# Channel norms: squares per tile on two engines, sums in four strips of the array, root and inverse on a column, tables loaded beside a norm

## Chip, cores and metric

One core of one Trainium2 chip runs the whole program: two layers of one kind of block and one hybrid layer, 256 tokens, width 1024, all in fp32. The metric is the device time of one execution in microseconds (us), less is better. Engines are called TensorE (PE; PEld is its weight load), VectorE (DVE), ScalarE (ACT), GpSimd (POOL) and SyncE (SP).

## The reference

The change touches only the norms over the 1024 channels of each token. In the reference they are:

```python
def rmsnorm(x, g):
    y = xf * lax.rsqrt(jnp.mean(xf * xf, axis=-1, keepdims=True) + NORM_EPS)
    return (y * g.astype(jnp.float32)).astype(x.dtype)

def layernorm(x, g, b):
    mu = jnp.mean(xf, axis=-1, keepdims=True)
    var = jnp.mean(jnp.square(xf - mu), axis=-1, keepdims=True)
    return ((xf - mu) * lax.rsqrt(var + LN_EPS) * g + b).astype(x.dtype)

def modulate(x, g, shift, scale):
    return rmsnorm(x, g) * (1 + scale) + shift
```

Around them stand the mixers (a recurrence over tokens, a convolution, gates), the choice and the weighted sum of 16 x 8 expert rows per token (`peer`), and in the hybrid layer four attention-like branches and an MLP.

## The kernel before

Activations lie with channels on partitions: a tensor of 1024 channels and 256 tokens is 8 tiles of 128 partitions x 256 tokens. The mean over channels is therefore a sum over partitions and tiles, made on TensorE with a 128x128 matrix of ones as the stationary operand; the sum then stands in all 128 partitions.

The program is a row of stages (`k.stage()`, line 82). Each stage opens a block in which every engine has its own list of instructions; at its end all engines meet, and the counters' marks are taken again. Within a stage engines wait for each other only through counters (`multiplied`, `vec_step`, `act_step`). Nothing of one stage runs beside the next, except DMAs and gathers that a stage has issued and not waited for.

`channel_norm` (line 356) is one such stage. ScalarE squares all tiles in one instruction (line 398). TensorE multiplies the 8 tiles of squares by ones into one PSUM bank (line 416). VectorE scales and adds eps over 128x256 (line 381), ScalarE takes the root (400), VectorE the reciprocal (385), and then VectorE multiplies tile by tile (387) while ScalarE follows with gain and shift, tile by tile (404). With `center=True` the mean comes first: 8 matmuls (411), a scaling (374), and one subtraction over all tiles (375). It is called 17 times: in the opening without gain (line 2510), for the mixers (1338) and the experts (1510) with gain and shift, three times centred after the convolution (1318), twice on one or two tiles (2268, 2269), and with a gain alone at 2302, 2365, 2367, 2375 and 2625.

In three places a job of expert rows is hosted beside other work: GpSimd gathers rows into a ring of four (`fetch_rows`, 1462), and VectorE uses a fixed number of them at the start of each stage (`use_rows`, 1440; in a norm four, or two when centred). `k.job` is None where none is hosted.

`gemm` (line 111) multiplies a weight of n blocks with the activations; its first four blocks are fetched by the stage before. Products follow most norms, and cannot start before the norm's stage has ended. In the opening (2479) SP has queued the tables of the modulation, the layer's tables and x before the norm; TensorE then multiplies the modulation's tables with 32-column weights, each of four tables onto its own 32 rows of a PSUM bank, in turn (`multiply`, 270).

`load` (line 345) is a stage of its own: SP issues transfers and waits for them, and all other engines wait at its end. It is used for `final_g` (in `k_final`, 2655), for the second table of constants (program) and for three small tables of the second block (2296).

## Time and profile before

| | us |
|---|---|
| median of 3 runs | 6153.47 |
| lowest, highest | 6142.9, 6162.07 |
| the profiled execution, its own time | 6142.74 |
| its span, first to last instruction | 6140.9 |
| TensorE busy (matmuls) | 3304.5 (54%) |
| VectorE busy | 3687.1 (60%) |
| ScalarE busy | 1000.6 (16%) |
| GpSimd busy | 1843.9 (30%) |
| granted TensorE clock, mean | 0.749 of full |

How to read it: the shares are averages over stages in which different engines work, so no share tells what a stage is bound by. In the page's list of groups, `L416` is the line of the kernel, `x246` the number of records (an fp32 matmul leaves two), then busy us and mean ns of one, and behind the bar how long the engine had been idle before them and whom it had waited for. A timeline shows single instructions (or merged neighbours) in order of time. `PEclk` is the granted clock of TensorE; 1.00 is 2.4 GHz and 0.50 is 1.2 GHz.

### The profile page before, as it was taken

How to read it: one execution, taken by the hardware profiler on the slowest of the kernel's cores; microseconds unless marked ns; L12 is line 12 of the kernel's file. 1: busy time of each engine (PE TensorE's matmuls, PEld its weight loads, DVE VectorE, ACT ScalarE, POOL GpSimd, SP SyncE). 2: the span in 40 equal slices, each digit the busy share in tenths (PEclk: the TensorE clock that was granted, in tenths of full speed). 3: DMA queues.
4: the chain of work that ended last, by engine and by line, in shares of the span. 5: the costliest groups of instructions: out<-in, count | busy, mean ns of one | idle time of the engine just before them, and what ended most of it. 6: DMA issues, size and time to landing. Idle time of an engine off the chain costs nothing. (4 is left out here: it accounts for less than half of the span.)

```text
span 6140.9 us, 90198 instructions
## 1 busy us (share of the span) xinstructions
PE 3304.5 (54%) x34040; PEld 2815.9 (46%) x34040; DVE 3687.1 (60%) x6974; ACT 1000.6 (16%) x2443; POOL 1843.9 (30%) x1550
## 2 busy tenths in 40 slices
PE   7688784887765013666500388878000000745988
PEld 6577673676654012556400367767000000644777
DVE  3556517568876866688799525661887898143110
ACT  1124211113330000233200012431000000111110
POOL 0000001326543750165577300000188776000000
PEclk9899997897687556777655689999555555866999
DMA  6320045767756971477799632003199998200432
GB/s 247 126 70 3 9 144 212 264 223 238 231 196 227 358 257 57 164 246 247 239 370 369 227 103 86 3 9 117 73 331 326 347 373 300 93 0 28 135 114 117
DMA packets 299017, 1117.17 MB, mean 182 GB/s; under 512 B 33696, under 2 KB 39088, under 8 KB 290224
## 3 DMA queue, kind: packets, MB, share of 16 engines
q0 software_dynamic: 221184, 805.40, 36.8%
q1 hardware_dynamic: 77488, 306.90, 14.6%
q8 instruction: 249, 4.08, 0.3%
q14 instruction: 96, 0.79, 0.0%
HBM read 1111.12 MB, written 1.05 MB: 181 GB/s over the span
## 5 line engine op out<-in xcount | busy, mean ns | idle before, releaser
L159 PE MATMUL psum<-h,weight_ring 128*128 128x256 f32 x4672 | 1045.0, 388 | 99.8 <-PEq L85 99.8
L1473 POOL DMA_INDIRECT ring<-in_peer_u,expert x496 | 620.4, 1251 | 1445.5 <-issue 667.4
L159 PEld LDWEIGHTS psum<-h,weight_ring 128*128 128x128 f32 x4672 | 909.5, 195 | 235.1 <-issue 101.0
L1715 DVE SCALAR_TENSOR_TENSOR tok<-ring,act,tok 128x1024 f32<-128x1024 f32 x688 | 884.0, 1285 | 94.1 <-DMA ring<-in_peer_v,expert_group 56.6
L1751 PE MATMUL psum<-constants,tok 128*128 128x128 f32 x48 | 10.7, 417 | 1564.5 <-PEq L85 1564.5
L1667 POOL DMA_INDIRECT ring<-in_peer_v,expert_group x688 | 776.8, 1129 | 219.4 <-issue 209.3
L1751 PEld LDWEIGHTS psum<-constants,tok 128*128 128x128 f32 x48 | 9.8, 225 | 1565.2 <-issue 1565.2
L1453 DVE CUSTOM_DVE_ANT_0 ring<-ring,tok 128x1024 f32<-128x1024 f32 x496 | 598.5, 1221 | 194.8 <-DMA ring<-in_peer_u,expert 175.4
L1667 POOL DMA_INDIRECT ring<-in_peer_u,expert_group x272 | 340.3, 1251 | 739.9 <-DVE expert_group L1703 662.2
L1710 DVE CUSTOM_DVE_ANT_0 ring<-ring,tok 128x1024 f32<-128x1024 f32 x272 | 329.7, 1226 | 85.7 <-DMA ring<-in_peer_u,expert_group 82.6
L159 PE MATMUL psum<-m,weight_ring 128*128 128x256 f32 x768 | 180.7, 401 | 53.5 <-PEq L85 53.5
L159 PEld LDWEIGHTS psum<-m,weight_ring 128*128 128x128 f32 x768 | 155.0, 203 | 79.2 <-issue 55.7
L398 ACT ACTIVATE squares<-x_tokens 128x2048 f32<-128x2048 f32 x7 | 13.4, 1910 | 1088.0 <-PEq L85 1088.0
L1266 PE MATMUL psum<-h,weight_ring 128*128 128x256 f32 x768 | 175.2, 391 | 23.5 <-PEq L85 23.5
L1018 POOL MEMSET W<- 128x1024 f32 x4 | 3.8, 953 | 595.0 <-POOLq L85 595.0
L416 PE MATMUL psum<-squares,constants 128*128 128x256 f32 x246 | 87.2, 529 | 170.9 <-ACT squares L398 170.9
L381 DVE TENSOR_SCALAR row<-psum 128x256 f32<-128x256 f32 x17 | 7.2, 424 | 280.4 <-PE psum L416 280.4
L1266 PEld LDWEIGHTS psum<-h,weight_ring 128*128 128x128 f32 x768 | 150.5, 197 | 47.4 <-issue 25.9
L574 ACT ACTIVATE E<-psum 128x256 f32<-128x256 f32 x288 | 110.7, 384 | 268.0 <-PE psum L599 261.8
L416 PEld LDWEIGHTS psum<-squares,constants 128*128 128x128 f32 x246 | 66.0, 276 | 190.9 <-ACT squares L398 177.1
L1473 POOL DMA_INDIRECT ring<-in_peer_v,expert x80 | 96.6, 1208 | 153.4 <-DVE tok L1457 136.5
L1216 DVE SCALAR_TENSOR_TENSOR zc<-u,vec,zc 128x256 f32<-128x256 f32 x336 | 133.3, 475 | 0.0
(510 smaller groups left out, 6451.1 us busy)
## 6 DMA issues: line engine op xcount, KB each, us to landing
weight_ring<-in_w_in SPq DMA_DIRECT2D x228, 512.0 KB, 3.6
ada_ring<-in_ada_w SPq DMA_DIRECT2D x40, 1024.0 KB, 8.8
weight_ring<-in_w_q SPq DMA_DIRECT2D x48, 512.0 KB, 3.5
weight_ring<-in_w_out SPq DMA_DIRECT2D x32, 512.0 KB, 3.6
weight_ring<-in_w_gate SPq DMA_DIRECT2D x32, 512.0 KB, 3.7
weight_ring<-in_w_mlp_in SPq DMA_DIRECT2D x32, 512.0 KB, 3.5
weight_ring<-in_w_mlp_out SPq DMA_DIRECT2D x8, 2048.0 KB, 7.6
weight_ring<-in_w_oB SPq DMA_DIRECT2D x24, 512.0 KB, 3.7
```

What stands on the lines that cost most here:

```text
L159: mm = pe.matmul(k.bank(slot, tokens), ring[:, slot, j * P:j * P + P], rhs(j), start=(j == 0), stop=(j == w.kt - 1))
L398: act.activation(squares[:], dst if center else src, ACT.Square).then_inc(k.act_step.up(), 1)
L416: mm = pe.matmul(total, k.ones, squares[:, j, :], start=(j == 0), stop=(j == tiles - 1))
L574: act.activation(out[:, g], product(q, g), ACT.Copy).then_inc(k.act_step.up(), 1)
L1216: ins = dve.scalar_tensor_tensor(conv[:, j, :], src, w, conv[:, j, :], ALU.mult, ALU.add)
L1266: mm = pe.matmul(k.bank(slot, 256), k.ring[:, slot, j * P:j * P + P], rhs(j), start=(j == 0), stop=(j == 7))
L1453: ins = dve.tensor_tensor_reduce(row, row, job.tok[:, tile, :], 1.0, 0.0, ALU.mult, ALU.add, dot)
L1473: pool.indirect_dma_start(job.ring[:, r % HOSTED, :], None, job.tables[kind], bass.IndirectOffsetOnAxis(ap=job.eidx[:, number:number + 1], ...
L1667: pool.indirect_dma_start(r.ring[:, j, :], None, table, bass.IndirectOffsetOnAxis(ap=idx8[part][:, j:j + 1], axis=0),).then_inc(k.gathered ...
L1710: dve.tensor_tensor_reduce(r.ring[:, j, :], r.ring[:, j, :], job.tok[:, tile, :], 1.0, 0.0, ALU.mult, ALU.add, r.dot8[:, part, j:j + 1]).t ...
L1715: dve.scalar_tensor_tensor(job.tok[:, tile, :], r.ring[:, j, :], r.act8[:, part, j:j + 1], job.tok[:, tile, :], ALU.mult, ALU.add).then_in ...
L1751: mm = pe.transpose(k.psum[:, 256 * j + P * i:256 * j + P * i + P], job.tok[:, i, P * j:P * j + P], k.ident)
```

## The change

`channel_norm` is rewritten. Squares are made tile by tile; in a norm that isn't centred and hosts no job, every second tile in the new order is squared by VectorE, the others by ScalarE. Sums are made with 32 columns of ones: tiles 2b and 2b+1 go to strip b of the array and so to partitions 32b to 32b+31 of PSUM, and the order changes strip with every matmul. TensorE waits for each tile's square on its own. VectorE copies the four partial sums to SBUF (`parts`). Two matmuls with `parts` as weights and a new table `band_rows` (a one in partitions 0, 32, 64, 96; 4 columns) add the strips and bring tokens onto partitions: the sum for 256 tokens is then a column of 2 numbers per partition. Mean, eps, root and reciprocal work on that column. Two matmuls with the column broadcast as weights and the identity as data spread it as a row over all partitions, in PSUM. The products read this row from PSUM. With a gain alone, gain and row are applied in one VectorE instruction, and ScalarE has no part in it. A centred norm sums its mean in strips too; ScalarE copies and scales the parts, one matmul adds and spreads them, and the subtraction is done tile by tile.

`channel_norm` can also carry loads: SP issues them and waits for them in the norm's stage. The second constants and the second block's three tables are loaded so beside the final norm of the first block, and `final_g` at the very start, behind x.

```diff
--- before.py
+++ after.py
@@ -353,39 +353,52 @@
             sp.wait_ge(k.loaded.sem, k.loaded.count)
-def channel_norm(k, src, dst, tiles, width, eps, mul=None, add=None, center=False, tokens=256):
-    nc = k.nc
+def channel_norm(k, src, dst, tiles, width, eps, mul=None, add=None, center=False, tokens=256, loads=()):
+    bands = min(4, tiles)
+    depth, halves, used = tiles // bands, tokens // P, slice(0, 32 * bands)
+    order = [band * depth + n for n in range(depth) for band in range(bands)]
+    shared = not center and k.job is None
+    on_vector = order[1::2] if shared else []
     with (
         k.sbuf("squares", [tiles, tokens]) as squares,
-        k.sbuf("row", [tokens]) as row,
+        k.sbuf("parts", [tokens]) as parts,
+        k.sbuf("column", [halves]) as column,
         k.stage() as block,
     ):
-        total, mean = k.bank(0, tokens), k.bank(1, tokens)
-        marks = {}
+        mean_parts, mean, total_parts, turned, row = k.bank(0, tokens), k.bank(1, tokens), k.bank(2, tokens), k.bank(3, 4 * halves), k.bank(4, tokens)
+        marks, squared = {}, {}
+        base = dst if center else src
+        if loads:
+            @block.sync
+            def _(sp):
+                for to, table in loads:
+                    sp.dma_start(to, table).then_inc(k.loaded.up(16), 16)
+                sp.wait_ge(k.loaded.sem, k.loaded.count)
         @block.vector
         def _(dve):
             chain = chained(k, dve)
-            base = src
             use_rows(k, dve, 2 if center else 4)
+            for j in on_vector:
+                dve.tensor_tensor(squares[:, j, :], src[:, j, :], src[:, j, :], ALU.mult).then_inc(k.vec_step.up(), 1)
+                squared[j] = k.vec_step.sem, k.vec_step.count
             if center:
-                dve.wait_ge(k.multiplied.sem, k.multiplied.at(1))
-                chain(dve.tensor_scalar(row[:], mean, 1.0 / width, None, ALU.mult))
-                chain(dve.tensor_tensor(dst, src, over_tiles(row[:], tiles, tokens), ALU.subtract))
-                base = dst
-            marks["centered"] = k.vec_step.count
-            n = 2 if center else 1
+                dve.wait_ge(k.multiplied.sem, k.multiplied.at(2))
+                for j in order:
+                    dve.tensor_tensor(dst[:, j, :], src[:, j, :], mean, ALU.subtract).then_inc(k.vec_step.up(), 1)
+                    marks["centered", j] = k.vec_step.count
+            n = 3 if center else 1
             dve.wait_ge(k.multiplied.sem, k.multiplied.at(n))
-            chain(dve.tensor_scalar(row[:], total, 1.0 / width, eps, ALU.mult, ALU.add))
+            dve.tensor_copy(parts[used, :], total_parts[used, :]).then_inc(k.vec_step.up(), 1)
+            marks["parts"] = k.vec_step.count
+            dve.wait_ge(k.multiplied.sem, k.multiplied.at(n + 1))
+            sums = turned.rearrange("p (i c) -> p i c", c=4)[:, :, 0]
+            chain(dve.tensor_scalar(column[:], sums, 1.0 / width, eps, ALU.mult, ALU.add))
             marks["variance"] = k.vec_step.count
-            dve.wait_ge(k.act_step.sem, k.act_step.at(2))
-            chain(dve.reciprocal(row[:], row[:]))
-            for j in range(tiles):
-                dve.tensor_tensor(dst[:, j, :], base[:, j, :], row[:], ALU.mult).then_inc(k.vec_step.up(), 1)
-            marks["normed"] = k.vec_step.count
         @block.gpsimd
         def _(pool):
@@ -394,26 +407,67 @@
         @block.scalar
         def _(act):
             if center:
-                act.wait_ge(k.vec_step.sem, marks["centered"])
-            act.activation(squares[:], dst if center else src, ACT.Square).then_inc(k.act_step.up(), 1)
+                act.wait_ge(k.multiplied.sem, k.multiplied.at(1))
+                act.activation(parts[used, :], mean_parts[used, :], ACT.Copy, scale=1.0 / width).then_inc(k.act_step.up(), 1)
+            for j in order:
+                if j in on_vector:
+                    continue
+                if center:
+                    act.wait_ge(k.vec_step.sem, marks["centered", j])
+                act.activation(squares[:, j, :], base[:, j, :], ACT.Square).then_inc(k.act_step.up(), 1)
+                squared[j] = k.act_step.sem, k.act_step.count
             act.wait_ge(k.vec_step.sem, marks["variance"])
-            act.activation(row[:], row[:], ACT.Sqrt).then_inc(k.act_step.up(), 1)
-            for j in range(tiles if mul is not None else 0):
+            act.activation(column[:], column[:], ACT.Sqrt).then_inc(k.act_step.up(), 1)
+            marks["root"] = k.act_step.count
+        @block.vector
+        def _(dve):
+            dve.wait_ge(k.act_step.sem, marks["root"])
+            dve.reciprocal(column[:], column[:]).then_inc(k.vec_step.up(), 1)
+            marks["inverse"] = k.vec_step.count
+            dve.wait_ge(k.multiplied.sem, k.multiplied.at(5 if center else 3))
+            for j in range(tiles):
+                if mul is None or add is not None:
+                    ins = dve.tensor_tensor(dst[:, j, :], base[:, j, :], row, ALU.mult)
+                else:
+                    ins = dve.scalar_tensor_tensor(dst[:, j, :], base[:, j, :], mul[:, j:j + 1], row, ALU.mult, ALU.mult)
+                ins.then_inc(k.vec_step.up(), 1)
+            marks["normed"] = k.vec_step.count
+        @block.scalar
+        def _(act):
+            for j in range(tiles if add is not None else 0):
                 act.wait_ge(k.vec_step.sem, marks["normed"] - tiles + j + 1)
-                act.activation(dst[:, j, :], dst[:, j, :], ACT.Identity, scale=mul[:, j:j + 1], bias=0.0 if add is None else add[:, j:j + 1]
-                               ).then_inc(k.act_step.up(), 1)
+                act.activation(dst[:, j, :], dst[:, j, :], ACT.Identity, scale=mul[:, j:j + 1], bias=add[:, j:j + 1]).then_inc(k.act_step.up(), 1)
         @block.tensor
         def _(pe):
+            def banded(out, t, n, j):
+                band = slice(32 * (j // depth), 32 * (j // depth) + 32)
+                return pe.matmul(out[band, :], k.ones[:, 0:32], t[:, j, :], start=(n < bands), stop=(n >= tiles - bands))
             if center:
-                for j in range(tiles):
-                    mm = pe.matmul(mean, k.ones, src[:, j, :], start=(j == 0), stop=(j == tiles - 1))
+                for n, j in enumerate(order):
+                    mm = banded(mean_parts, src, n, j)
                 mm.then_inc(k.multiplied.up(), 1)
-            pe.wait_ge(k.act_step.sem, k.act_step.at(1))
-            for j in range(tiles):
-                mm = pe.matmul(total, k.ones, squares[:, j, :], start=(j == 0), stop=(j == tiles - 1))
+                pe.wait_ge(k.act_step.sem, k.act_step.at(1))
+                pe.matmul(mean, k.band_rows[used, 0:1].broadcast_to([32 * bands, P]), parts[used, :], start=True, stop=True).then_inc(k.multiplied.up(), 1)
+            for n, j in enumerate(order):
+                sem, value = squared[j]
+                pe.wait_ge(sem, value)
+                mm = banded(total_parts, squares, n, j)
+            mm.then_inc(k.multiplied.up(), 1)
+            pe.wait_ge(k.vec_step.sem, marks["parts"])
+            for i in range(halves):
+                mm = pe.matmul(turned[:, 4 * i:4 * i + 4], parts[used, P * i:P * i + P], k.band_rows[used, :], start=True, stop=True)
+            mm.then_inc(k.multiplied.up(), 1)
+            pe.wait_ge(k.vec_step.sem, marks["inverse"])
+            for i in range(halves):
+                mm = pe.matmul(row[:, P * i:P * i + P], column[:, i:i + 1].broadcast_to([P, P]), k.ident, start=True, stop=True)
             mm.then_inc(k.multiplied.up(), 1)
@@ -2293,11 +2347,15 @@
                   96 ** -0.5, k.chunk_causal, b.kv[:, 2:4, :], None, out)
-def second_block(k, dram, x):
+def second_tables(k, mem, dram):
+    c = buffers(k, mem, vec=[Layout(VECTORS2).width], rows=[12], gate_up=[P], h=[8, 256], branches=[4, 2, 256])
+    return c, [(c.vec[:], dram.vectors2), (c.rows[:], dram.rows2), (c.gate_up[0:16, :], dram.gate_up)]
+def second_block(k, dram, x, c):
     with ExitStack() as mem:
         lay = Layout(VECTORS2)
-        c = buffers(k, mem, vec=[lay.width], rows=[12], gate_up=[P], h=[8, 256], branches=[4, 2, 256])
-        load(k, (c.vec[:], dram.vectors2), (c.rows[:], dram.rows2), (c.gate_up[0:16, :], dram.gate_up))
         V = names(**{name: c.vec[:, a:z] for name, (a, z) in lay.at.items()})
         channel_norm(k, x[:], c.h[:], 8, 1024, 1e-6, V.norm_mix_pre_2)
@@ constants
+        "band_rows": np.broadcast_to(p % 32 == 0, (P, 4)),
@@ -2613,22 +2672,23 @@
         lay = Layout({n: a.shape[1] for n, a in constants().items()})
         table = ctx.enter_context(nc.sbuf_tensor("constants", [P, lay.width], F32))
...
         k.ring = ctx.enter_context(k.sbuf("weight_ring", [SLOTS_W, 8 * P]))
         x = ctx.enter_context(nc.sbuf_tensor("x_tokens", [P, 8, 256], F32))
+        final_g = ctx.enter_context(nc.sbuf_tensor("final_g", [P, 8], F32))
         with nc.sbuf_tensor("context_tokens", [P, 8, 256], F32) as xc:
-            first_block(k, dram, x, xc, [(table[:], dram.constants), (xc[:], dram.ctx)], [(x[:], dram.x)])
-        channel_norm(k, x[:], x[:], 8, 1024, 1e-6, k_final(k, ctx, dram))
-        k.dump("x_first", x[:])
+            first_block(k, dram, x, xc, [(table[:], dram.constants), (xc[:], dram.ctx)], [(x[:], dram.x), (final_g[:], dram.final_g)])
         lay2 = Layout({n: a.shape[1] for n, a in constants(of_second=True).items()})
         table2 = ctx.enter_context(nc.sbuf_tensor("constants_second", [P, lay2.width], F32))
-        load(k, (table2[:], dram.constants_second))
+        c, tables = second_tables(k, ctx, dram)
+        channel_norm(k, x[:], x[:], 8, 1024, 1e-6, final_g[:], loads=[(table2[:], dram.constants_second), *tables])
+        k.dump("x_first", x[:])
         (k.lo, k.up_incl, k.lo_incl, k.up8, k.lo8, k.up_far, k.upto, k.chunk0, k.chunk1, k.causal, k.chunk_causal, k.turn, k.cos, k.sin) = (table2[:, a:z] for a, z in lay2.at.values())
-        second_block(k, dram, x)
+        second_block(k, dram, x, c)
         with buffers_scope(k, rows=[2, 1024]) as s, k.stage() as block:
@@ -2650,15 +2710,6 @@
                 sp.dma_start(dram.out.rearrange("b (i p) c -> p (b i) c", p=P), s.rows[:]).then_inc(k.stored.up(16), 16)
                 sp.wait_ge(k.stored.sem, k.stored.count)
...
-    return g[:]
 def columns(v):
```

## Rows read from the trace of the kernel before

**Rows 1.** The page's costliest groups; columns: line, engine, operation, count, busy, mean ns, idle before.

```profile
L381 DVE TENSOR_SCALAR row<-psum 128x256 f32<-128x256 f32 x17 | 7.2, 424 | 280.4 <-PE psum L416 280.4
```

**Rows 2.** Timeline of one plain norm; columns: start, us, engine, line, operation, idle before.

```profile
828.76 1.91 ACT L398 ACTIVATE squares<-context_tokens 128x2048 f32<-128x2048 f32 x1 [1.11 <-PEq L85]
830.73 5.41 PE L416 MATMUL psum<-squares,constants 128*128 128x256 f32 x16 [3.59 <-ACT squares L398]
836.17 0.42 DVE L381 TENSOR_SCALAR row<-psum 128x256 f32<-128x256 f32 x1 [7.77 <-PE psum L416]
...
837.15 1.75 DVE L385 RECIPROCAL row<-row 128x256 f32<-128x256 f32 x1 [0.56 <-ACT row L400]
838.94 2.77 DVE L387 TENSOR_TENSOR h<-context_tokens,row 128x256 f32<-128x256 f32 x8
839.40 4.04 ACT L404 ACTIVATE h<-h,mod 128x256 f32<-128x256 f32 x8 [2.35 <-DVE h L387]
```

**Rows 3.** Timeline, first and last work of the first and third centred norm.

```profile
208.57 6.54 PE L411 MATMUL psum<-zc,constants 128*128 128x256 f32 x16 [23.85 <-PEq L85]
...
229.25 4.04 ACT L404 ACTIVATE m<-m,vec 128x256 f32<-128x256 f32 x8 [2.35 <-DVE m L387]
...
3603.21 3.69 PE L411 MATMUL psum<-zc,constants 128*128 128x256 f32 x16 [0.88 <-PEq L85]
...
3621.57 4.04 ACT L404 ACTIVATE m<-m,vec 128x256 f32<-128x256 f32 x8 [2.35 <-DVE m L387]
```

**Rows 4.** Timeline, the one matmul of the norm over one tile.

```profile
5522.80 1.22 PE L416 MATMUL psum<-squares,constants 128*128 128x256 f32 x2 [4.98 <-ACT squares L398]
```

**Rows 5.** Timeline of the opening: its norm, the modulation's strips and their transposes.

```profile
14.43 1.91 ACT L398 ACTIVATE squares<-context_tokens 128x2048 f32<-128x2048 f32 x1 [4.82 <-PEq L85]
...
27.73 6.45 PE L275 MATMUL psum<-ring,ada_c 128*32 128x256 f32 x64 [5.96 <-PEq L85]
...
34.68 0.44 PE L292 MATMUL psum<-constants,ada_rows 128*128 128x128 f32 x2 [0.50 <-ACT ada_rows L282]
...
35.05 3.66 PE L275 MATMUL psum<-ring,ada_c 128*32 128x256 f32 x64
```

**Rows 6.** Timeline, work elsewhere of the shapes that the prediction prices.

```profile
376.61 3.29 ACT L1042 ACTIVATE G<-z,vec 128x256 f32<-128x256 f32 x8
...
2259.33 3.22 DVE L1758 SCALAR_TENSOR_TENSOR context_tokens<-psum,gate,context_tokens 128x256 f32<-128x256 f32 x8 [3.85 <-PE psum L1751]
...
5392.84 0.99 PE L1946 MATMUL psum<-y,constants_second 128*128 128x4 f32 x4
...
5508.03 0.21 ACT L1879 ACTIVATE row<-row 128x8 f32<-128x8 f32 x1 [0.41 <-DVE row L1869]
```

**Rows 7.** Timeline, the last operation of a norm with a gain alone.

```profile
5858.36 3.30 ACT L404 ACTIVATE gate<-gate,vec 128x256 f32<-128x256 f32 x8 [2.35 <-DVE gate L387]
```

**Rows 8.** Timeline of a norm with hosted expert rows: start, last row, last operation.

```profile
1033.48 1.91 ACT L398 ACTIVATE squares<-x_tokens 128x2048 f32<-128x2048 f32 x1 [1.43 <-PEq L85]
...
1038.15 0.08 DVE L1453 DVE_READ_ACCUMULATOR2_ANT dots<- 128x1 f32 x1
...
1044.85 4.04 ACT L404 ACTIVATE h<-h,mod 128x256 f32<-128x256 f32 x8 [2.36 <-DVE h L387]
```

**Rows 9.** Busy us by window: PE, PEld, DVE, ACT, POOL, then PEclk, DMA share, GB/s.

```profile
36.00:39.00 3.00, 2.71 (x52) 1.37 (x44) 0.00 (x0) 0.22 (x1) 0.00 (x0) 1.00 0.90 363
...
849.20:853.00 3.80, 3.74 (x10) 3.06 (x11) 0.00 (x0) 0.00 (x0) 0.00 (x0) 0.55 0.02 4
```

**Rows 10.** Timeline around the final norm of the first block and the tables' loads.

```profile
5199.59 3.23 DVE L1758 SCALAR_TENSOR_TENSOR x_tokens<-psum,gate,x_tokens 128x256 f32<-128x256 f32 x8 [4.08 <-PE psum L1751]
...
5205.30 1.91 ACT L398 ACTIVATE squares<-x_tokens 128x2048 f32<-128x2048 f32 x1 [377.29 <-PEq L85]
...
5219.91 0.33 SPq L352 DMA_DIRECT2D constants_second<-in_constants_second  x1
...
5228.19 1.91 ACT L398 ACTIVATE squares<-x_tokens 128x2048 f32<-128x2048 f32 x1 [8.59 <-PEq L85]
```

More of the change, by code:

```diff
@@ L2615, in program @@
         (k.ident, k.ones, k.blocks64,
-         gram_up0, gram_up1, gram_lo0, gram_lo1, k.pair_ident, k.pair_up8, k.pair_lo8, k.pair_up_far, k.pair_lo_far, k.halves, k.quarters, k.head_rows, k.head_spread, k.segments, k.iota16) = (
+         gram_up0, gram_up1, gram_lo0, gram_lo1, k.pair_ident, k.pair_up8, k.pair_lo8, k.pair_up_far, k.pair_lo_far, k.halves, k.quarters, k.band_rows, k.head_rows, k.head_spread, k.segments, k.iota16) = (
             table[:, a:z] for a, z in lay.at.values())
@@ L2652, in _ @@
                 sp.wait_ge(k.stored.sem, k.stored.count)
-def k_final(k, ctx, dram):
-    g = ctx.enter_context(k.nc.sbuf_tensor("final_g", [P, 8], F32))
-    load(k, (g[:], dram.final_g))
-    return g[:]
 def columns(v):
```

## The prediction

> **What bounds the kernel now.** I read the page's engine shares first: no engine is near full over the span, so the time is a chain of stages, and what a change to the norms is worth is read inside the norms. The page's group of the variance instruction gives their number, 17, and that VectorE stood idle 280.4 us before them, always for the sums on TensorE [rows 1]. Next I read the timeline of one norm from its first to its last instruction [rows 2]. There nothing overlaps: Square over all 8 tiles (1.91 us), then 8 matmuls (5.41), the variance (0.42), the root (0.56 with its hand-overs), the reciprocal (1.75), the first product, and 8 scalings on ScalarE (4.04). It starts at 828.76 and ends at 839.40 + 4.04 = 843.44, so 14.68 us, in which every other engine waits. The stage's end is a barrier, and the next stage needs h, so a microsecond taken from this chain is taken from the kernel, unless something else ends last. I look for that something below: DMA in the first norm and the rows hosted beside two others.
>
> The 17 norms are: 12 plain ones of 8 tiles (one with no gain, in the opening; 6 with gain and shift, two of which host expert rows; 5 with a gain alone), 3 centred ones after the convolution, and 2 small ones (2 tiles and 1 tile) of the latent attention.
>
> **The prices I use.** A 128x128x256 fp32 matmul shows as two records. Eight of them take 3.69 us at 2.4 GHz [rows 3], so 0.46 each; a single one at 1.2 GHz takes 1.22 from start to end [rows 4], which is about 0.86 of work and 0.35 of latency.
> - Strips: the kernel has such matmuls already, in the modulation: 64 records (32 matmuls of 32 columns, on the four strips in turn) take 6.45 us at 1.2 GHz and 3.66 at 2.4 GHz [rows 5]. Eight of them are 1.6 and 0.9 us. In a norm they follow their squares, so only the last pair is exposed: two records on each of two strips, 2 x 0.43 + 0.3 = 1.15 us cold.
> - Turning the sums: two fp32 matmuls with 128 columns of weights and 4 of data, 4 records. Four records of just that shape take 0.99 us [rows 6]; 1.05 with the hand-over.
> - Spreading the inverse: two matmuls with 128 columns of data, 4 records. No row shows them alone; two transposes of 128 columns are 0.44 for 2 records [rows 5], so 4 are between 0.65 (warm) and 1.3 (the isolated matmul's 1.22 and a hand-over); I take 1.15, nearer to the cold one.
> - Squares by tile: 8 ScalarE instructions of that shape with a per-partition scale take 3.29 us [rows 6], 0.41 each. Four take 1.6; VectorE's four take 4 x 0.35 = 1.4 (2.77 / 8 in [rows 2]) and are done first.
> - The copy of the sums costs what the variance over 256 columns did, 0.42. The three steps on a column of two numbers: ScalarE's root of that kind is 0.21 [rows 6]; I take 0.2 for the two on VectorE and 0.15 for hand-overs, 0.76 in all, against 0.42 + 0.56 + 1.75 before.
> - The product with a row that lies in PSUM: 8 fused instructions of this form with a PSUM operand take 3.22 us [rows 6]. Where a shift follows, ScalarE's 4.04 still sets the end, and nothing changes there.
>
> **A plain norm after.** 1.6 (squares) + 0.04 + 1.15 (last pair) + 0.46 (copy) + 1.1 (turn) + 0.76 (column) + 1.2 (spread) = 6.3 us, and then 0.5 + 4.04 with a shift: 10.85. With a gain alone it is 3.3 instead: 9.65. Before, the first is 14.68 and the second 0.74 less (3.30 in place of 4.04, [rows 7]): 13.9. So:
> - 4 with gain and shift, no hosted rows: 3.8 each, 15.3 us.
> - 5 with a gain alone: 4.3 each where the sums ran mostly cold (3 of them), and 1.3 less in the 2 whose sums ran at 2.4 GHz throughout (the old matmuls take 3.7 there, as the warm ones of [rows 3], so 1.7 less, and the new last pair 0.4 less): 12.9 + 6.0 = 18.9.
> - 2 with hosted rows: VectorE first uses four rows, until 1038.2, 4.75 after the start [rows 8], and takes no squares. ScalarE's eight are done after 3.3 us and the sums after 4.4, so the copy starts at 4.8, when the rows are done. End: 4.8 + 0.42 + 1.1 + 0.76 + 1.2 + 4.54 = 12.8 against 1044.85 + 4.04 - 1033.48 = 15.4: 2.6 each, 5.2. Nothing is queued behind the copy that the rows need: their next gathers depend on the rows used, which come first as before.
> - The first norm ends without ScalarE; it began at 14.43, and the next stage's first matmul came at 27.73 [rows 5], 12.9 without the stage change. It becomes 9.3: 3.6 less. What could take its place is the DMA of the modulation's tables, of x and of the first weights. The DMA engines are busy to 0.90 even from 36 to 39 us [rows 9], and are done then. The tables' last strips, which ended at 35.05 + 3.66 = 38.7, would end at 35.1; the modulation and 8 scalings of 4.04 us come after them, so the first product would start at about 41.5, still behind the last transfer. final_g now stands behind x in that queue; it is 4 KB. I count 3.6, with 0 as the other end.
> - 3 centred: before 229.25 + 4.04 - 208.57 = 24.7 us cold, and 3621.57 + 4.04 - 3603.21 = 22.4 where the first sums ran warm [rows 3]. After: strip sums 2.0 (warm 1.25), ScalarE's copy 0.42, one matmul that adds and spreads the mean 1.25 (0.7), first subtraction 0.45, 8 squares at ScalarE's pace 3.3, last pair 1.2, then the same tail of 0.46 + 1.1 + 0.76 + 1.2 + 4.54. That is 16.7 and 15.3: 8.0 + 2 x 7.1 = 22.2.
> - 2 small: there is little to spread over strips, and the new tail of three hops on TensorE costs about what the reciprocal gives back. The bounds are a gain of 0.9 and a loss of 0.3 each; I take 0.5 for both.
>
> **The loads.** final_g's stage disappears: VectorE ended at 5199.59 + 3.23 = 5202.82 and Square started at 5205.30, where a stage change costs 0.35: 2.1 us. The tables' two stages lie between 5219.91 and 5228.19 [rows 10]: 8.3 us. They now run beside the final norm: SP issues four transfers and then waits for them in the norm's own stage. All of it took 8.3 us with one wait in the middle, about 6 without, and the norm takes 9.65, so it is hidden. Were the cover too short, the most that comes back is 8.3. Sum: 10.4.
>
> **Sum.** 15.3 + 18.9 + 5.2 + 3.6 + 22.2 + 0.5 + 10.4 = 76 us. The profiled execution took 6142.7 us (span 6140.9), which is the lowest of the times shown; their median is 6153.5. So 6142.7 becomes 6067, and the median 6077.
>
> **Two rules beside the rows.** The trace's own strips run at four times one full matmul (0.115 us against 0.46, [rows 3, 5]). The Trainium skill, "TensorE: Matmul & The Clock Gate", section "Measured speedup vs the span model", gives 2.38 for three column tiles, which would be about 3.1 for four; with it the last pair would cost 0.3 us more a norm, and the sum would be about 71. The trace disagrees, and I go by it. Against this change speaks a rule in "TensorEngine Tiling (Array Packing)", where it says that a change of tiling mode drains the array: a norm now goes from full array to strips and back. Here full-width transposes at 34.68 last until 35.12 while the strips' first record starts at 35.05 [rows 5], so no drain of a size that matters shows.
>
> **Rivals.**
> 1. The clock stays at 2.4 GHz through the norm. For it: the old sums often ended warm, and the next product starts cold after the long quiet tail (granted clock 0.55 in its first 3.8 us, [rows 9]). With a shorter norm the clock may not fall. That gives up to 1.3 us more in each of 15 norms and up to 2 us at some ten product starts: 20 to 40 us more, 6035 to 6058. Against it: TensorE has four short bursts and a pause of 4.5 us before the product. Chance 0.13.
> 2. Part comes back. The small steps (turning, spreading, a column through three engines, three more waits) may cost more than their nearest rows, 0.3 to 0.5 us at each of six hand-overs, or the hosted norms' 12 us may be waited out on gathers. That leaves 30 to 60 us: 6095 to 6125. Chance 0.12.
> 3. The strips don't run side by side when each waits for its own square. Then 8 matmuls at 0.86 us end 7.3 us after the start instead of 2.8: 4.5 for 11 norms, 3.5 for 2, 8 for 3, which is 80 us, the whole gain: about 6155, no change. Against it: consecutive matmuls here change strip each time, as in [rows 5]. Chance 0.03.
> 4. Slower than before: the product after each norm is paid for by the norm's thin TensorE work. Before, its first blocks ran at 1.2 GHz for about 4 us. If the bursts left the clock low for longer, each microsecond costs half a microsecond; the 76 us are used up when the 14 products behind norms stay low 11 us longer each, and beyond that the kernel is slower, 6155 to 6180. Against it: the old kernel's products rose after 4 us although TensorE had been quiet before them for the whole tail of the norm, 7 us and more. Chance 0.03.
>
> **How the numbers follow.** My own forecast, 6058 to 6095, has 0.69. Predicted is 6077. From 6045 to 6108 I leave out the far half of rival 1 and of rival 2 and all of 3 and 4, about 0.18. A measurement can tell about 0.3%, 18 us: below 6135 lie my forecast and rivals 1 and 2, 0.94; rival 3 and the top of 2 are no change, 0.03; slower 0.03.
>
> **What would show it.** Right: the timeline of a plain norm has its last strip record about 2.8 us after its start and its last ScalarE instruction at 10.9 (9.7 for a gain alone); centred norms of 15 to 17 us; Square of the norm behind the final one directly after it, with SP's waits inside the final norm; the first product at about 41.5. Wrong: the strip records in a row instead of side by side; turning or spreading over 1.5 us; a root that waits for its table load (it is issued after the last square and has 2.5 us to be hidden in, and lasts 1.28); a granted clock that is still 0.5 more than 6 us into the next product.

## Result and the profile of the changed kernel

The changed kernel takes 6063.9 us (median; 6046.2 to 6076.3) where the kernel before, run beside it, takes 6157.8 (6142.9 to 6165.6). The ratio is 0.9848, with a 95% interval of 0.9816 to 0.9880: 94 us less, between 74 and 113. The forecast was 76 us less, with a range of 6058 to 6095 us for the time.

The profiled execution of the changed kernel took 6076.26 us and is the slowest of its four; the one of before was the fastest of its own. Their spans, 6072.7 and 6140.9, are therefore only 68 us apart, and the norms are better read one by one. First the page's head and shares of the changed kernel (busy us, share of the span, instructions of each engine) and its group of ScalarE's squares:

```profile
span 6072.7 us, 90542 instructions
...
PE 3268.7 (54%) x34182; PEld 2775.8 (46%) x34182; DVE 3680.5 (61%) x7050; ACT 976.6 (16%) x2468; POOL 1866.8 (31%) x1550
...
L417 ACT ACTIVATE squares<-x_tokens 128x256 f32<-128x256 f32 x32 | 10.6, 404 | 1092.3 <-PEq L85 1092.3
```

The engines are as far from full as before. Next the timeline of the norm that answers to [rows 2] (start, us, engine, line, operation, idle before and what ended it):

```profile
812.60 1.34 ACT L417 ACTIVATE squares<-context_tokens 128x256 f32<-128x256 f32 x4 [1.11 <-PEq L85]
812.62 1.43 DVE L386 TENSOR_TENSOR squares<-context_tokens 128x256 f32<-128x256 f32 x4 [0.39 <-PEq L85]
...
813.07 1.67 PE L447 MATMUL psum<-squares,constants 128*32 128x256 f32 x16 [2.10 <-ACT squares L417]
814.77 0.42 DVE L396 COPY parts<-psum 128x256 f32<-128x256 f32 x1 [0.71 <-PE psum L447]
...
815.25 0.61 PE L465 MATMUL psum<-constants,parts 128*128 128x4 f32 x4 [0.52 <-DVE parts L396]
815.89 0.16 DVE L400 TENSOR_SCALAR column<-psum 128x2 f32<-128x2 f32 x1 [0.70 <-PE psum L465]
816.09 0.20 ACT L420 ACTIVATE column<-column 128x2 f32<-128x2 f32 x1 [2.15 <-DVE column L400]
816.32 0.17 DVE L426 RECIPROCAL column<-column 128x2 f32<-128x2 f32 x1 [0.27 <-ACT column L420]
...
816.54 0.71 PE L470 MATMUL psum<-constants,column 128*128 128x128 f32 x4 [0.68 <-DVE column L426]
817.29 2.74 DVE L431 TENSOR_TENSOR h<-context_tokens,psum 128x256 f32<-128x256 f32 x8 [0.80 <-PE psum L470]
817.75 4.04 ACT L441 ACTIVATE h<-h,mod 128x256 f32<-128x256 f32 x8 [1.46 <-DVE h L431]
```

It ends at 817.75 + 4.04 = 821.79: 9.19 us, against 14.68. Square over all tiles and the sums behind it (7.4 us in [rows 2]) have become 2.14 us in which ScalarE's squares, VectorE's squares and the sums overlap, and the reciprocal of 1.75 has become 0.17. What did not change is the last row, 4.04 us of ScalarE, now 44% of the norm.

TensorE's part of this norm ran at 2.4 GHz, which is called warm below; cold is 1.2 GHz. In the norm behind the final one TensorE ran cold (same columns):

```profile
5177.99 1.34 ACT L417 ACTIVATE squares<-x_tokens 128x256 f32<-128x256 f32 x4 [5.10 <-PEq L85]
...
5178.46 2.29 PE L447 MATMUL psum<-squares,constants 128*32 128x256 f32 x16 [4.10 <-ACT squares L417]
...
5181.26 1.02 PE L465 MATMUL psum<-constants,parts 128*128 128x4 f32 x4 [0.52 <-DVE parts L396]
...
5182.97 1.22 PE L470 MATMUL psum<-constants,column 128*128 128x128 f32 x4 [0.69 <-DVE column L426]
5184.23 3.22 DVE L433 SCALAR_TENSOR_TENSOR h<-x_tokens,vec,psum 128x256 f32<-128x256 f32 x8 [1.31 <-PE psum L470]
```

The windows by engine over both norms, and over the product behind each, show the granted clock beside them (busy us of PE, PEld, DVE, ACT, POOL, then PEclk, DMA share, GB/s):

```profile
812.60:815.30 2.70, 1.72 (x17) 0.93 (x17) 1.86 (x5) 1.34 (x4) 0.00 (x0) 1.00 0.45 174
817.30:821.80 4.50, 0.00 (x0) 0.00 (x0) 2.73 (x8) 4.04 (x8) 0.00 (x0) 0.68 0.00 0
5178.00:5181.00 3.00, 2.29 (x16) 1.24 (x16) 1.65 (x5) 1.33 (x4) 0.00 (x0) 0.50 0.02 5
5187.80:5192.00 4.20, 4.15 (x11) 3.41 (x12) 0.00 (x0) 0.00 (x0) 0.00 (x0) 0.57 0.00 0
827.40:833.80 6.40, 6.36 (x18) 5.23 (x19) 0.00 (x0) 0.00 (x0) 0.00 (x0) 0.59 0.00 0
```

The sums of the first norm are at 1.00 and those of the second at 0.50 of full clock. In the tail of the first norm, where TensorE does nothing, the granted clock falls (0.68 in the mean), and both products start low, as before in [rows 9].

All 17 norms, from first to last instruction, in order of time within a row (below, norm 3 is the third norm of the program, and so on; 3, 6, 8, 10 have gain and shift, 11, 12, 15, 16, 17 a gain alone, 4 and 7 host rows, 2, 5, 9 are centred):

| norms | before, us | after, us | gained | forecast |
|---|---|---|---|---|
| first | 12.92 | 8.98 | 3.9 | 3.6 |
| 4 gain and shift | 14.68, 15.09, 14.59, 14.67 | 9.19, 10.72, 10.73, 9.20 | 19.2 | 15.3 |
| 5 gain alone | 14.30, 14.80, 12.25, 14.01, 12.25 | 9.46, 9.46, 7.91, 9.46, 7.92 | 23.4 | 18.9 |
| 2 with hosted rows | 15.41, 15.45 | 12.60, 12.58 | 5.7 | 5.2 |
| 3 centred | 24.75, 22.58, 22.43 | 16.00, 13.28, 13.25 | 27.2 | 22.2 |
| 2 small | 6.93, 5.46 | 6.21, 5.47 | 0.7 | 0.5 |
| loads outside norms | 2.48, 8.59 | 0.35, 0.37 | 10.4 | 10.4 |
| start of the first norm | 14.43 | 16.80 | -2.4 | 0 |

Together 88 us: 80.2 in the norms, 10.4 from the loads, less 2.4. The timeline of SyncE's queue and of ScalarE in the opening shows the last line of that table, which answers to [rows 5]:

```profile
12.05 2.11 SPq L2553 DMA_DIRECT2D x_tokens<-in_x  x1
14.20 2.11 SPq L2553 DMA_DIRECT2D final_g<-in_final_g  x1
...
16.80 1.33 ACT L417 ACTIVATE squares<-context_tokens 128x256 f32<-128x256 f32 x4 [7.02 <-PEq L85]
```

Why are the two spans only 68 us apart? The three stretches in which gathered expert rows run freely took 1436 us in this execution of the changed kernel and 1412 in the one of before. The waits of VectorE on those gathers (us in total, times, longest), in the changed kernel:

```profile
DVE ring L1764 <- DMA ring<-in_peer_u,expert_group: 95.4, 138, 4.9
DVE tok L1769 <- DMA ring<-in_peer_v,expert_group: 65.9, 129, 4.8
```

and in the kernel before:

```profile
DVE ring L1710 <- DMA ring<-in_peer_u,expert_group: 82.6, 112, 4.8
DVE tok L1715 <- DMA ring<-in_peer_v,expert_group: 56.6, 120, 4.6
```

With these 24 us back, the span's difference is 92. That they belong to the change is unlikely: the profiles of the experiments below, which all hold most of it, have the same stretches at 1404 to 1426 us. A second profile of the kernel before was taken to see how far they vary without the change.

> The kernel before, unchanged, for a second profile of it. The profile of the changed kernel shows the three stretches of free-running row gathers 24 us longer in sum (1436 us) than the profile of before (1412) and than the four variants so far (1408 to 1410). Theory: that is spread between executions and not the change; this profile has 1400 to 1440 us, and 17 norms of 252.6 us in sum as in the first. Rival: the change does something to the gathers; then all executions of before stay at or below 1412 and this one says nothing against it.

It took 6139.5 us (span 6137.7). The gather stretches took 1405 us; that is the side of 1412 on which its rival has it too, so this profile by itself does not decide. What speaks for spread are the variants: seven kernels that keep the rewritten norm or most of it are at 1404 to 1426. Why the changed kernel's one profile has 1436 stays open. The norms of the second profile sum to 248.7 us instead of 252.6; two of them ran 1.7 and 1.5 us shorter at the higher clock (12.99 and 21.07). So a norm's own length varies by up to 1.7 us with the clock between executions of one kernel. The rest of the program varies as well. Outside the gather stretches, the norms and the loads, the five experiments that have the changed kernel's code there (all but the two with filling) take 11 to 25 us more than the changed kernel's own profile. That 88 us by norms, 92 by spans and 94 by medians lie so close is therefore in part luck.

### The profile page after: what moved, and what is told of

It reads as the page before. It is cut to its first block and busy times, and to the rows that moved or that the text cites. A ratio compares the mean times of both kernels' runs of the same rounds, so it can differ in the third digit from the quotient of the medians.

```text
span 6072.7 us, 90542 instructions
## 1 busy us (share of the span) xinstructions
PE 3268.7 (54%) x34182; PEld 2775.8 (46%) x34182; DVE 3680.5 (61%) x7050; ACT 976.6 (16%) x2468; POOL 1866.8 (31%) x1550
## 5 line engine op out<-in xcount | busy, mean ns | idle before, releaser
L159 PEld LDWEIGHTS psum<-h,weight_ring 128*128 128x128 f32 x4672 | 903.7, 194 | 208.1 <-issue 79.2
L1721 POOL DMA_INDIRECT ring<-in_peer_u,expert_group x272 | 353.4, 1299 | 736.6 <-DVE expert_group L1757 658.8
L1511 DVE SCALAR_TENSOR_TENSOR tok<-ring,dots,tok 128x1024 f32<-128x1024 f32 x80 | 102.9, 1287 | 48.3 <-DMA ring<-in_peer_v,expert 44.6
L653 PE MATMUL psum<-E,E 64*64 64x64 f32 x3072 | 112.4, 222 | 19.1 <-DVE E L607 16.5
```

The source lines that it names most:

```text
L159: mm = pe.matmul(k.bank(slot, tokens), ring[:, slot, j * P:j * P + P], rhs(j), start=(j == 0), stop=(j == w.kt - 1))
L653: mm = pe.matmul(product(q, g)[h, n, :], left[h, g, n, :], rhs, start=True, stop=True)
L1511: ins = dve.scalar_tensor_tensor(job.tok[:, tile, :], row, dot, job.tok[:, tile, :], ALU.mult, ALU.add)
L1721: pool.indirect_dma_start(r.ring[:, j, :], None, table, bass.IndirectOffsetOnAxis(ap=idx8[part][:, j:j + 1], axis=0),).then_inc(k.gathered ...
```

## Experiments

Each ratio is against the kernel before, run on the same chip in the same session (its median is 6145.2 us for the runs on loads, final_g, one strip and the warm tail, 6147.8 for the others; beside the changed kernel it was 6157.8, so two variants are better compared by their ratios than by their medians). All diffs are against the changed kernel.

**The loads put back into stages of their own.**

```
-            first_block(..., [(x[:], dram.x), (final_g[:], dram.final_g)])
+            first_block(..., [(x[:], dram.x)])
...
-        channel_norm(k, x[:], x[:], 8, 1024, 1e-6, final_g[:], loads=[(table2[:], dram.constants_second), *tables])
+        load(k, (final_g[:], dram.final_g))
+        channel_norm(k, x[:], x[:], 8, 1024, 1e-6, final_g[:])
+        load(k, (table2[:], dram.constants_second))
+        load(k, *tables)
```

> The changed kernel, with only its loads as they were before: final_g in a stage of its own in front of the final norm, and the second constants and the three small tables in two stages behind it. The norms stay rewritten. Theory: the loads' part of the change is worth 8.3 us behind the final norm and 2.1 us in front of it, but 2.4 us of that are lost in the opening, where SP spends 2.11 us on the issue of final_g (16.80 instead of 14.43 us for the first Square). So this kernel should be 8 us longer than the changed one, all of it between the end of the first block and the next norm, and its first Square should come at 14.4 us again. Rival: issuing final_g cost nothing and the late first Square was something else; then the first Square stays at 16.8 and the difference is 10.4 us.

Measured: 6057.9 us, ratio 0.9854 [0.9824, 0.9884]. The timeline at the final norm:

```profile
5165.18 0.33 SPq L352 DMA_DIRECT2D constants_second<-in_constants_second  x1
...
5173.39 1.34 ACT L417 ACTIVATE squares<-x_tokens 128x256 f32<-128x256 f32 x4 [13.30 <-PEq L85]
```

The gap before the next norm is 8.56 us again instead of 0.37, and the first norm starts at 14.47 instead of 16.80. Both are as the theory of the loads has them; the norms sum to 172.2 (172.4 in the changed kernel). The time cannot tell the net 8 us: 0.9854 and 0.9848 are the same within their intervals. The effect is seen in the profile alone.

**final_g issued first instead of last.**

```
-            first_block(k, dram, x, xc, [(table[:], dram.constants), (xc[:], dram.ctx)], [(x[:], dram.x), (final_g[:], dram.final_g)])
+            first_block(k, dram, x, xc, [(final_g[:], dram.final_g), (table[:], dram.constants), (xc[:], dram.ctx)], [(x[:], dram.x)])
```

> The changed kernel, with final_g as the first of the opening's transfers instead of the last. Theory: the 2.4 us that the first norm starts later come from the last issue on SP, which takes 2.11 us because the transfers queued before it fill the queue; issued first it costs 0.4 us, so the first Square comes at about 14.9 us and the kernel is 2 us shorter. Rival: any further transfer costs its 2.1 us wherever it stands in the list, and nothing changes (16.8 us).

Measured: 6056.5 us, 0.9854 [0.9817, 0.9892]. The opening's timeline:

```profile
0.76 0.40 SPq L2549 DMA_DIRECT2D final_g<-in_final_g  x1
...
12.32 2.11 SPq L2553 DMA_DIRECT2D x_tokens<-in_x  x1
...
14.91 1.34 ACT L417 ACTIVATE squares<-context_tokens 128x256 f32<-128x256 f32 x4 [4.61 <-PEq L85]
```

The same transfer of 4 KB costs 0.40 us of issue at 0.76 us and 2.11 at 14.20, and the first norm starts 1.9 us earlier. It is the place in the queue, not the norm's new form, that delayed it. Two microseconds are again below what the time tells.

**One strip instead of four.**

```
-    bands = min(4, tiles)
+    bands = 1
```

> The changed kernel, with all tiles of a norm summed in one strip of 32 columns instead of four (the order of tiles then no longer changes strip). Theory: strips are worth what they overlap. Eight matmuls in one strip take 0.86 us each at 1.2 GHz and 0.43 at 2.4 GHz one after the other, so the sums end at 7.6 us (4.2) instead of 2.7 (2.1). Cold norms get 4 to 5 us longer, those that start warm 2, centred ones 4, hosted ones 3: 50 us in all. Rival: the squares' pace sets the sums, and strips matter little; then the kernel is at most 10 us longer.

Measured: 6104.3 us, 0.9935 [0.9916, 0.9954], and the norms sum to 208.1 us, 35.7 more. The sums of a warm and of a cold norm, then the spread of the cold one:

```profile
823.62 3.64 PE L447 MATMUL psum<-squares,constants 128*32 128x256 f32 x16 [2.10 <-ACT squares L417]
...
3439.66 6.05 PE L447 MATMUL psum<-squares,constants 128*32 128x256 f32 x16 [4.09 <-ACT squares L417]
...
3447.50 0.71 PE L470 MATMUL psum<-constants,column 128*128 128x128 f32 x4 [0.69 <-DVE column L426]
```

On four strips the sums took 1.67 and 2.29. The strips thus do run side by side, each while the others still wait for their squares, and they carry 36 us in the profile; by the ratios it is 0.9 points, 54 us, and this is the one part that the time alone tells from the changed kernel. The rival by which the squares' pace sets the sums falls. The 50 us expected were too many for two reasons. In the norms that start cold the clock rises during the longer sums, and the spread behind them takes 0.71, not 1.22. And the two hosted norms grew by 0.1 and 0.6 where 3 each was expected: their rows hold VectorE for 4.7 us in any case, and turn and spread ran warm behind the late sums.

**All squares on ScalarE.**

```
-    shared = not center and k.job is None
+    shared = False
```

> The changed kernel, with all eight squares of every norm on ScalarE, none on VectorE. Theory: in the ten norms that share them, the last square then ends at 2.6 us instead of 1.4, since ScalarE makes one in 0.33 us, and the sums' end follows it. Each of these norms gets 1.0 to 1.3 us longer, 10 to 13 us in all; centred and hosted norms stay as they are. Rival: the sums end with TensorE's own pace on the strips and not with the last square; then the norms grow by less than 0.5 us each, 5 us in all.

Measured: 6071.3 us, 0.9869 [0.9842, 0.9895]; norms 182.1 us, 9.7 more. The squares of the warm norm and their sums:

```profile
814.50 2.56 ACT L417 ACTIVATE squares<-context_tokens 128x256 f32<-128x256 f32 x8 [1.11 <-PEq L85]
...
814.97 2.77 PE L447 MATMUL psum<-squares,constants 128*32 128x256 f32 x16 [2.10 <-ACT squares L417]
```

Eight squares follow each other at 0.31 us here, so the second engine saves 1.2 us of squares and 1.1 of sums. Eight of the ten shared norms grew by 0.9 to 1.1 us, 8.1 together; the other two not, as they ran at a higher clock than in the changed kernel. Two norms that the edit does not touch changed with the clock too: a centred one is 2.6 us longer (15.91 against 13.28; TensorE was quiet for 2.27 us before its second sums, against 0.99, and they ran cold) and a hosted one 0.9 shorter. With all ten at one clock the sharing would be worth about 10 us, an estimate from the eight, at the lower end of the 10 to 13 expected. The time alone does not separate it. The rival falls: the sums follow the last square.

**Root and inverse on rows of 256 again, with the new sums.** One matmul adds the strips and spreads the total; the root, the reciprocal and the products use the row.

```
-            chain(dve.tensor_scalar(column[:], sums, 1.0 / width, eps, ALU.mult, ALU.add))
+            chain(dve.tensor_scalar(line[:], row, 1.0 / width, eps, ALU.mult, ALU.add))
...
-            act.activation(column[:], column[:], ACT.Sqrt).then_inc(k.act_step.up(), 1)
+            act.activation(line[:], line[:], ACT.Sqrt).then_inc(k.act_step.up(), 1)
...
-            dve.reciprocal(column[:], column[:]).then_inc(k.vec_step.up(), 1)
+            dve.reciprocal(line[:], line[:]).then_inc(k.vec_step.up(), 1)
...
+            pe.matmul(row, k.band_rows[used, 0:1].broadcast_to([32 * bands, P]), parts[used, :], start=True, stop=True).then_inc(k.multiplied.up(), 1)
```

> The changed kernel, without the turn to a column: one matmul with the band table broadcast as weights adds the strips' parts and spreads them over all partitions as a row of 256, and mean with eps, root and reciprocal work on 128x256 as before the change; the products read the row from SBUF. Theory: the column pays. It costs 1.02 + 1.22 us on TensorE in a cold norm (0.61 + 0.71 in a warm one) and 0.7 for its three small steps; the row costs 1.22 (0.70) on TensorE and 0.42 + 0.42 + 0.1 + 1.75 after it. So each of the 17 norms gets 0.9 to 1.4 us longer, 20 us in all. Rival: the column only moves the reciprocal's time to TensorE and hand-overs; then the sums differ by less than 0.3 us a norm, 5 us in all.

Measured: 6075.2 us, 0.9874 [0.9847, 0.9900]; norms 190.6 us, 18.2 more. Its timeline in the same warm norm:

```profile
827.74 0.70 PE L462 MATMUL psum<-parts,constants 128*128 128x256 f32 x2 [0.52 <-DVE parts L396]
828.47 0.42 DVE L399 TENSOR_SCALAR line<-psum 128x256 f32<-128x256 f32 x1 [0.79 <-PE psum L462]
828.93 0.42 ACT L419 ACTIVATE line<-line 128x256 f32<-128x256 f32 x1 [2.50 <-DVE line L399]
829.38 1.75 DVE L425 RECIPROCAL line<-line 128x256 f32<-128x256 f32 x1 [0.48 <-ACT line L419]
831.16 2.77 DVE L429 TENSOR_TENSOR h<-context_tokens,line 128x256 f32<-128x256 f32 x8
```

From the matmul to the first product it is 3.42 us on rows; on the column it is 817.29 - 815.25 = 2.04, with one trip to TensorE and one hand-over more. The column form wins 1.4 us warm and 1.0 cold, so it is worth its hops: 18 of the 80 us in the norms, where 20 were expected. This too is read from the profile: the intervals of the two ratios overlap.

**TensorE kept busy over the norm's tail.** Matmuls that nobody reads fill the time while ScalarE writes the last tiles.

```
             mm.then_inc(k.multiplied.up(), 1)
+            for _ in range((5 if add is not None else 4) if tiles == 8 else 0):
+                pe.matmul(k.bank(5, 256), k.ones, k.segments[:, 0:256], start=True, stop=True)
```

> The changed kernel, with five matmuls (four where no shift follows) of 128x128x256 into a PSUM bank that nobody reads, issued behind the two that spread the inverse in each norm of 8 tiles. They run while VectorE and ScalarE write the norm's result. Theory A: the product behind a norm starts at 1.2 GHz only because TensorE is quiet in that tail; with the filling its first block takes about 3.8 us instead of 5.6 to 6.3, in 14 products, and the kernel gets 20 to 28 us shorter. Theory B: the clock doesn't follow such a short filling; the first blocks stay at 5.6 us and more, and the kernel is the same. If the matmuls delayed the stage's end (at 1.2 GHz five take 4.3 us against a tail of 4.5), norms would get longer by up to 0.5 us.

Measured: 6047.4 us, 0.9844 [0.9812, 0.9875], no different from the changed kernel's 0.9848. The timeline behind one norm where it worked:

```profile
3430.66 3.27 PE L473 MATMUL psum<-constants 128*128 128x256 f32 x10
...
3439.59 0.38 ACT L177 ACTIVATE zc<-psum 128x256 f32 x1 [4.19 <-PE psum L159]
```

The product started at 3435.76, and its first block (the first 128 rows of its result) was copied out of PSUM 3.83 us later; in the changed kernel that takes 5.2 to 6.4. But of the 11 products whose first block is that slow in the changed kernel only 4 did so. The timeline of TensorE in the norm behind the final one, in this kernel, and its windows show a case where it didn't:

```profile
5147.93 1.66 PE L447 MATMUL psum<-squares,constants 128*32 128x256 f32 x16 [1.21 <-ACT squares L417]
...
5151.95 1.89 PE L473 MATMUL psum<-constants 128*128 128x256 f32 x8
```

```profile
5147.40:5150.20 2.80, 1.75 (x17) 0.97 (x17) 1.86 (x5) 1.34 (x4) 0.00 (x0) 1.00 0.00 0
5155.70:5160.00 4.30, 4.22 (x12) 3.46 (x13) 0.00 (x0) 0.00 (x0) 0.00 (x0) 0.60 0.01 4
```

Through the matmuls of the norm before it, this norm ran at full clock (7.92 us instead of 9.46), but its product began at 0.60: the filling had ended at 5151.95 + 1.89 = 5153.84, and the product came at 5155.78. In three more places the sub-keys' load, a stage of its own, lies between norm and product, and in three the gate of the convolution; the product comes 6.4 to 8.6 us after the filling there, and it starts low. So the mechanism is right and the size was not: the 11 first blocks together are 8 us shorter, of the 20 to 28 expected, and the time does not show it.

**The version that the experiments point to.** final_g first; the sub-keys loaded beside the norm in front of them; filling sized for each norm (4 to 9 matmuls), and 6 in the stage of the convolution's gate, whose product also waits for ScalarE.

```
+def keep_warm(k, pe, n):
+    for _ in range(n):
+        pe.matmul(k.bank(5, 256), k.ones, k.segments[:, 0:256], start=True, stop=True)
...
-        channel_norm(k, x, b.h[:], 8, 1024, 1e-6, mod.scale2, mod.shift2)
+        channel_norm(k, x, b.h[:], 8, 1024, 1e-6, mod.scale2, mod.shift2, loads=[(b.keys[:], dram.sub_keys[l])], fill=fill)
```

> A version that may beat both. The changed kernel, with final_g first in the opening; the experts' sub-keys (1 MB, three times in a stage of their own behind a norm, 5.3 us each) loaded beside that norm; and filling matmuls that nobody reads sized to the clock that each norm showed: 9 in the tail of norms that run at 2.4 GHz, 5 or 4 in cold ones, 7 in the norm behind the final one, and 6 in the stage behind each centred norm. Theory: 16 us from the keys, 2 from final_g, and about 2 us for each of 11 products that now start at 2.4 GHz (first block 3.8 us instead of 5.2 to 6.8), 22: 40 us shorter than the changed kernel. Theory B (the clock doesn't follow where the norm was cold or where the filling ends over a microsecond before the product): 18 + 8 us.

Measured: 6018.8 us (6006.5 to 6030.1), 0.9782 [0.9755, 0.9809]. It beats both kernels; its interval lies below that of the changed kernel, and 0.66 points are 41 us. The timeline at the norm of [rows 2], then its windows:

```profile
807.66 0.33 SPq L384 DMA_DIRECT2D keys<-in_sub_keys  x1
...
812.16 4.05 PE L359 MATMUL psum<-constants 128*128 128x256 f32 x18
...
812.82 4.04 ACT L447 ACTIVATE h<-h,mod 128x256 f32<-128x256 f32 x8 [1.46 <-DVE h L437]
...
821.05 0.39 ACT L177 ACTIVATE q<-psum 128x256 f32 x1 [4.19 <-PE psum L159]
```

```profile
812.00:816.80 4.80, 4.21 (x21) 3.40 (x20) 2.73 (x8) 3.98 (x8) 0.00 (x0) 1.00 0.17 67
816.80:821.00 4.20, 3.78 (x18) 3.37 (x19) 0.00 (x0) 0.06 (x1) 0.00 (x0) 1.00 0.00 0
```

From the norm's start to the product it is 9.6 us, where it was 14.8 in the changed kernel (812.60 to 827.44), and the first block takes 3.83 instead of 6.37. Three norms have the sub-keys, 16 us; the first blocks gave 22, final_g 2, and warmer norms 1.7: 42 us by the profiles. The 41 us by the ratios agree, but by the two intervals they are uncertain by some 25 us, so that closeness is luck. How the filling and the keys share this was read from the profile and not timed apart.

## Why the prediction was right, point by point

- **What bounds the kernel: right.** What came out of the norms came out of the kernel: 88 us by the tables above, 94 by the medians. The sum had 76, so it was 12 too low, 14.5 in the norms less 2.4 at the start; the time still lies in the range. Of the 80 us in the norms the experiments take back 62 to 64: strips 36, sharing of squares 8 to 10, column 18. The remaining 16 to 18 (sums that begin with the first square, the subtraction by tile, gain and row in one instruction) no run took back.
- **Strips: right in mechanism and size.** Last record 2.76 us after a cold start, where 2.8 was forecast. Without the other three strips the norms are 36 us longer. Rival 3 falls; it was also priced too high, 80 us for what one strip showed to be 36.
- **Squares by tile: mis-sized.** "0.41 each" was taken from instructions with a per-partition scale; without it four take 1.34, and eight 2.56 to 2.74 instead of 3.3. This is 0.6 us in each centred norm; in the shared norms the squares are done after 1.45 us, at VectorE's pace, instead of 1.6.
- **Turn, column, spread: right when cold.** 1.02, then 0.16 + 0.20 + 0.17 and hand-overs, then 1.22, against 1.1, 0.76 and 1.2. Cold norms came out at 10.72 and 9.46 where 10.85 and 9.65 were forecast.
- **The clock inside the norm: the term that failed.** The sum treated turn and spread as cold in every norm, "1.1 (turn)" and "1.2 (spread)". In the changed kernel TensorE stays at 2.4 GHz to the end of six norms, and there these take 0.61 and 0.71. Norms 3 and 10 gained 5.5 each instead of 3.8, norms 15 and 17 gained 4.3 instead of 3.0, and two centred ones (5 and 9) 9.3 and 9.2 instead of 7.1. These six hold 10.3 of the 14.5 us by which the norms beat their forecast. About 8 of the 10.3 are the clock: a warm norm is 1.5 us shorter than a cold one (9.19 against 10.72, 7.91 against 9.46) and a centred one 2.7 (13.28 against 16.00), of which the sum had counted 0, 0.4 and 1.4. The rest are the squares and small terms.
- **Rival 1** (the clock stays up): half of it came true, within the norm. What TensorE did before goes with it. In norms 3 and 10 the first sum now comes after 2.10 us of quiet, and in the changed kernel and all seven variants both stay warm to the end; before, it came after 3.59, started warm, and the clock fell during the sums in three of four cases. In norms 5 and 9 the second sums come after 0.99 and 0.96 us, against 4.78 before. In the cold norm above it is 4.10. A short quiet keeps the clock but does not raise it: norm 2 of the changed kernel, cold from its start, has 0.96 there and stays cold. That quiet is the cause is supported by the fillers, which made norm 12 warm at 1.21 us of quiet; where the line lies no run shows. The other half of the rival, the product behind the norm, did not come true: the first blocks took 5.2 to 6.4 us where they had taken 5.2 to 6.8. The "pause of 4.5 us before the product" was read right only for five of these 11 products (3.7 to 4.9 us); for the other six it is 10.2 to 10.8, since the sub-keys' load or the convolution's gate lies between.
- **Hosted norms: right.** The copy starts at 1016.02, directly behind the fourth row, 4.67 after the start (4.8 forecast), and the norm takes 12.6 (12.8).
- **First norm and final_g: half right.** The norm is 3.9 shorter, and no DMA took its place. But "final_g now stands behind x in that queue; it is 4 KB" priced the transfer by its bytes and not the issue by its row: 2.1 us, all in front of the first norm. The first product starts at 42.94, not at 41.5; it was 45.19, so the kernel gained 2.3 us there and not 3.6.
- **Centred norms: right in form.** 16.0 where 16.7 was forecast, and 13.3 where 15.3 was, by the two terms above.
- **Small norms, loads: right**, 0.7 for 0.5 and 10.35 for 10.4. The four issues take 1.8 us, inside the norm.
- **Rival 2** (part comes back) gave nothing: the new waits cost 0.03 to 0.06 us each. **Rival 4** neither: the 11 first blocks sum to 64.7 us, against 67.3 and 68.9 in the two profiles of the kernel before.
- The rest of the difference, 94 by the medians against 88 by the profiles, lies within the interval; 2.6 of it are these first blocks, the rest is not assigned.

## What to carry to other kernels

Where a stage is a chain through engines that wait for each other, write out its timeline, cut the steps into tiles so that they overlap, and bring small results into the layout in which they are short: a reciprocal of 2 columns is 0.17 us, of 256 it is 1.75. Price a shortened stage at both clock levels: less quiet before a burst can keep it at the higher one, as it did in four norms here, and two that were warm already were warm in their new steps too. When a load is moved, price its issue at the place in the queue where it will stand, not by its bytes.

## What the runs showed of the hardware

- The first three issues on SyncE's queue take 0.40 to 0.43 us each, and the last three, behind the big transfers, 2.11, the one of 4 KB (final_g) like the one of 1 MB (x).
- Sixteen records on four strips take 1.67 us while squares arrive (warm); 16 on one strip take 3.64. For strips whose data is ready, [rows 3, 5] have 0.115 us against 0.46 for one matmul, a factor of 4.0. The Trainium skill, "TensorE: Matmul & The Clock Gate", section "Measured speedup vs the span model", has a measured speedup of 2.38 for three column tiles; by that rule the strips would have been slower, and the trace disagrees.
- From full array to strips and back, the hand-over is 0.05 to 0.06 us (813.02 to 813.07, 815.19 to 815.25), as between any two engines here. The Trainium skill, "TensorEngine Tiling (Array Packing)", section "Key Properties", says that a change of tiling mode drains the array; no such time is seen in these rows, where the array has nothing in flight.
- After filling of 1.89 us and 1.9 us of quiet, a product started at 0.60 of the clock; after filling of 4.05 us and 1.01 of quiet it started at 1.00, and after 3.27 and 1.83 its first block was as short as that. Quiet alone does not tell the cases apart; what does was not tried.
